# Order of the token tiles in the projection matmuls of a fp32 transformer trunk

## The reference, cut to what matters

```python
def short_conv_mixer(h, w_in, conv_w, w_out):            # layer 0, latent and context tokens
    b_gate, c_gate, v = jnp.split(h @ w_in, 3, axis=-1)
    u = c_gate * v
    up = jnp.pad(u, ((0, 0), (1, 1), (0, 0)))
    z = conv_w[0] * up[:, :-2] + conv_w[1] * up[:, 1:-1] + conv_w[2] * up[:, 2:]
    return (b_gate * z) @ w_out

def swiglu(h, w_in, w_out):                              # both layers; FFN_HIDDEN = 2816
    gate, up = jnp.split(h @ w_in, 2, axis=-1)
    return (jax.nn.silu(gate) * up) @ w_out
```

## Time and profile before

| What | Value |
|---|---|
| Median of 3 runs | 3048.2 us (3044.87 to 3049.11) |
| Profiled execution: span, first to last instruction | 3040.4 us |
| What lies around the span (median less span) | 7.8 us |
| Mean granted TensorE clock over the span | 0.982 |
| TensorE matmul busy | 2898.9 us, 95% |
| VectorE busy | 1954.0 us, 64% |
| ScalarE busy | 866.6 us, 29% |
| GpSimd busy | 921.6 us, 30% |
| conv and ffn0 steps lie at | about 101 to 1481 us of the span |

### The profile page before, as it was taken

How to read it: one execution, slowest core, us unless ns; L and a number is a source line. 1 busy time by engine, 2 the same in 40 slices (tenths; PEclk the granted TensorE clock), 3 DMA queues, 4 the chain that set the end, 5 groups by cost and what they waited for, 6 DMA issues and landing times.

```text
span 3040.4 us, 45152 instructions
## 1 busy us (share of the span) xinstructions
PE 2898.9 (95%) x15546; PEld 2431.6 (80%) x15546; DVE 1954.0 (64%) x3260; ACT 866.6 (29%) x1537; POOL 921.6 (30%) x615
## 2 busy tenths in 40 slices
PE   4999999999999999999999899999798999999997
PEld 2888887788888888888789788888676878888885
DVE  3776775776667666744551566666614887777777
ACT  3211111411111111111241466666623222222222
POOL 1112111111111111112111344545421456565652
PEclk7999999999999999999999899999999999999998
DMA  7122214022221222111055565555640111111111
GB/s 295 46 66 83 72 55 93 32 65 75 72 78 57 78 77 78 52 42 41 35 154 130 151 177 155 168 151 146 191 144 28 42 42 48 55 48 55 48 55 63
DMA packets 178773, 269.43 MB, mean 89 GB/s; under 512 B 70656, under 2 KB 122880, under 8 KB 178688
## 3 DMA queue, kind: packets, MB, share of 16 engines
q1 hardware_dynamic: 178688, 268.32, 28.8%
HBM read 222.13 MB, written 50.07 MB: 90 GB/s over the span
## 4 chain that ended last, share of the span: by engine, by line
PE 78%; DVE 9%; issue 5%; ACT 3%; DMA 3%; POOL 1%; SPq 1%; DVEq 0%; ACTq 0%; POOLq 0%
PE psum L797 33%; PE psum L835 20%; PE psum L1167 5%; PE psum L1025 5%; PE psum L980 4%; PE psum L1079 2%; PE psum L1048 2%; PE psum L823 2%; PE psum L1062 2%; DVE residual L1724 1%; DVE prod_lo L2086 1%; DMA o_dram<-o_st_lo 1%; PE psum L884 1%; DVE part L2080 1%; PE psum L728 1%
## 5 line engine op out<-in xcount | busy, mean ns | idle before, releaser
L1724 DVE SCALAR_TENSOR_TENSOR residual<-psum,modulation,residual 128x512 f32<-128x512 f32 (+1 forms) x1072 | 715.6, 688 | 584.7 <-PE psum L835 581.4
L2174 POOL TENSOR_TENSOR w_lo<-raw,w_hi 128x1024 fp32r<-128x1024 f32 x158 | 396.6, 2521 | 1484.5 <-ACT w_hi L1217 1481.8
L835 PE MATMUL psum<-prod_hi,w_hi 128*128 128x512 f32 (+1 forms) x1072 | 403.6, 377 | 21.8 <-DVE residual L1724 7.3
L797 PE MATMUL psum<-act_hi,w_hi 128*128 128x512 f32 (+1 forms) x1608 | 405.4, 359 | 6.2 <-POOL w_lo L2192 4.3
L797 PE MATMUL psum<-act_lo,w_hi 128*128 128x512 f32 (+1 forms) x1608 | 405.3, 359 | 0.0
L797 PE MATMUL psum<-act_hi,w_lo 128*128 128x512 f32 (+1 forms) x1608 | 405.0, 358 | 0.0
L835 PE MATMUL psum<-prod_hi,w_lo 128*128 128x512 f32 (+1 forms) x1072 | 395.7, 369 | 0.0
L835 PE MATMUL psum<-prod_lo,w_hi 128*128 128x512 f32 (+1 forms) x1072 | 394.9, 368 | 0.0
L1217 ACT ACTIVATE w_hi<-raw 128x1024 fp32r<-128x1024 f32 x158 | 165.8, 1062 | 712.1 <-PE psum L797 607.3
L797 PEld LDWEIGHTS psum<-act_hi,w_hi 128*128 128x128 f32 x1608 | 284.5, 188 | 61.1 <-issue 4.9
L797 PEld LDWEIGHTS psum<-act_hi,w_lo 128*128 128x128 f32 x1608 | 268.0, 188 | 47.1
(11 more groups left out here) (205 smaller groups left out, 5148.6 us busy)
## 6 DMA issues: line engine op xcount, KB each, us to landing
raw<-ffn_panels SPq DMA_DIRECT2D x132, 512.0 KB, 3.8
mod_in<-mod_rest SPq DMA_DIRECT2D x64, 384.0 KB, 3.1
raw<-conv_panels SPq DMA_DIRECT2D x32, 512.0 KB, 5.3
mod_raw<-mod_panels SPq DMA_DIRECT2D x24, 512.0 KB, 8.2
more_row<-mod_panels SPq DMA_DIRECT2D x48, 256.0 KB, 2.8
k_hi<-k_dram SPq DMA_DIRECT2D x32, 320.0 KB, 5.7
k_lo<-k_dram SPq DMA_DIRECT2D x32, 320.0 KB, 7.3
v_st<-v_dram SPq DMA_DIRECT2D x32, 320.0 KB, 7.1
```

The costliest lines, as they stand in the source:

```text
L797: mm = pe.matmul(psum[:, bank + b, 0:tn], w[:, s, kb, :], acts[h][:, kb, t0:t0 + tn], start=(kb == 0 and n == 0), stop=(kb == KB - 1 and n ...
L835: mm = pe.matmul(psum[:, 6 + r % 2 if bank is None else bank, 0:tn], w[:, s, ob, :], h[:, t0:t0 + tn], start=(n == 0), stop=(n == 2))
L1724: dve.scalar_tensor_tensor(out=residual[:, ob, t0:t0 + tn], in0=psum[:, 6 + r % 2 if bank is None else bank, 0:tn], scalar=modulation[:, g ...
L2174: pool.tensor_tensor(panel(w_lo, s), raw[:, s], panel(w_hi, s), ALU.subtract).then_inc(lo_done[s], 1)
```

## The change

In `project` the loop over channel blocks is run twice: first for the two 512-column tiles (`numbered[:len(LAT)]`), with the out pieces and what else `extra` issues behind each channel block as before, and then for what is left (`numbered[len(LAT):]`), the 256-column context tile, with nothing between. Over `LAT` the second pass is empty. The waits on `early_lo` and `lo_done` in the first pass stay where they were in the channel-block order. The number of matmuls, their operands and their accumulation order within a tile are the same. The other engines' programs are not touched.

```diff
-                for kb in range(KB):
-                    if early is not None and kb == 0:
-                        pe.wait_ge(early_lo, early)
-                    elif early is not None and kb == KQ:
-                        pe.wait_ge(lo_done[s], base[phase][s] + i + 1)
-                    for n, (w, h) in enumerate(((w_hi, 0), (w_hi, 1), (w_lo, 0))):
-                        for b, (t0, tn) in enumerate(tiles):
-                            mm = pe.matmul(psum[:, bank + b, 0:tn], w[:, s, kb, :], acts[h][:, kb, t0:t0 + tn],
-                                           start=(kb == 0 and n == 0), stop=(kb == KB - 1 and n == 2))
-                            if kb == KB - 1 and n == 2:
-                                mm.then_inc(ready, 1)
-                    extra(kb)
+                numbered = list(enumerate(tiles))
+                for some in (numbered[:len(LAT)], numbered[len(LAT):]):
+                    for kb in range(KB):
+                        if early is not None and some[:1] == numbered[:1] and kb == 0:
+                            pe.wait_ge(early_lo, early)
+                        elif early is not None and some[:1] == numbered[:1] and kb == KQ:
+                            pe.wait_ge(lo_done[s], base[phase][s] + i + 1)
+                        for n, (w, h) in enumerate(((w_hi, 0), (w_hi, 1), (w_lo, 0))):
+                            for b, (t0, tn) in some:
+                                mm = pe.matmul(psum[:, bank + b, 0:tn], w[:, s, kb, :], acts[h][:, kb, t0:t0 + tn],
+                                               start=(kb == 0 and n == 0), stop=(kb == KB - 1 and n == 2))
+                                if kb == KB - 1 and n == 2:
+                                    mm.then_inc(ready, 1)
+                        if some[:1] == numbered[:1]:
+                            extra(kb)
```

## The result

The changed kernel takes 3065.94 us (median of 4 runs, 3065.45 to 3068.55) against 3048.65 (4 runs, 3044.87 to 3051.82) for the kernel before: a ratio of 1.0062, 95% interval 1.005 to 1.0074. By the two medians that is 17.3 us slower, by the ratio 18.9. The forecast was 3062.6, in a range of 3051 to 3077.

What follows compares the result with a forecast made beforehand. TensorE, with matmuls busy for 95% of the span, was taken to set the time. Terms of -13.2, +24.5, +2 and +1.1 us sum to +14.4, giving 3062.6 us on the median, range 3051 to 3077.

Steps and rivals of the forecast that it cites:

- Term 1: Matmul spacing in conv and ffn0: 1512 triples (two wide matmuls, one narrow) each 0.0087 us shorter, 13.2 us less.
- Rival B: Matmul spacing in conv and ffn0 doesn't change: sum +27.6 us, 3076 us; chance 0.10.
- Term 2: Out piece 11 of 16 group steps, after projection b's start E: wait 1.88 instead of 0.35 us, 24.5 us more.
- "line 1853 runs through": Bound of Term 2: GpSimd holds only line 1856's instructions; wait at piece 11 about 1.4 us, 16.8 us more.
- Rival A: Head of projection b: GpSimd doesn't hold VectorE, 3039 us, chance 0.09; halfway, only line 1856 held, 3055 us, 0.11.
- Term 3: Conv step starts: projection a waits for the late context copy, 0.45 us more in six steps; together 2 us more.
- Term 4: Start of ffn0 steps: piece 0's cover for w_lo of panel 2 shrinks but holds; last step 1.1 us more.
- Rival C: The clock falls in the new idle stretch of 1.7 us in group steps: 26 us, sum 3089 us; chance 0.08.
- the 7.8 us: Whole kernel before: median of the runs lies 7.8 us above the profiled span of 3040.4 us.

Runs made afterwards that it cites:

- grouped: Kernel before the change, one pass kept, but each channel block takes its six wide matmuls and then its three narrow ones: 3028.5 us, ratio 0.9945.
- the cover given back: Changed kernel with the out pieces of the last channel block issued behind the context pass instead of ahead of it: 3063.03 us, ratio 1.0046.

## Why the prediction was right, and where its sizes were off

**What bounds the kernel, and the sign.** Right. TensorE sets the time, its instructions are unchanged, and the result is spacing gained against waits added.

**Term 1, spacing (13.2 less).** Mis-sized. A plain step fell by 0.35 us, not 0.42; over its 48 triples that is 0.0073 each and 1512 x 0.0073 = 11.0 us. Start to start, two wide matmuls take 0.457 in the changed kernel's plain steps and not the 0.453 of the attention's output; the narrow ones are at 0.120 as forecast. Why wide ones are a little slower here is open. Rival B (no gain) is out: in the plain step nothing else was touched. The formula that rival B took from the Trainium skill (TensorE: Matmul & The Clock Gate, "Back-to-back issue gap") makes the gap depend on width alone, and the page calls it the gap of an isolated matmul. For the streams here the traces contradict it, with 0.582 us a triple before, 0.577 after and 0.575 to 0.576 grouped.

**Term 2, piece 11 (24.5 more).** The mechanism is right in each moment: `w_lo` forecast from E + 1.61 to 4.02 and measured at 1.61 to 4.01, modulation from E + 2.31 against 2.34, piece 11 at E + 6.34 against 6.33, its wait 1.88 against 1.84. Both halves of its growth, the later `w_lo` and the earlier due time, stand in the prediction's working. The cost was a little higher. A group step grew by 1.29 net; with the spacing gain of 0.35 taken out that is 1.64, not 1.53, and 16 x 1.64 = 26.2. The wait itself grew by 1.49. Starting again behind it costs some 0.1 us, but it cost that before as well. The other 0.15 is lost at piece 21, in every group step of the changed kernel and in none before. The prediction had cost the second placement of four modulation instructions, behind piece 17, at nothing. Behind it, the add of piece 19 ends at 1082.54, when piece 21 wants that bank, and the first matmul of piece 21 is followed after 0.34 us; before, it was free 0.8 us ahead and the distance was 0.23. The trace names no releaser for so short a wait; the times fit. DVE and PE after, then before:

```profile
1081.13 1.41 DVE L1727 SCALAR_TENSOR_TENSOR residual<-psum,modulation,residual 128x512 f32<-128x512 f32 x2
1082.59 0.50 PE L838 MATMUL psum<-prod_hi,w_hi 128*128 128x512 f32 x1
1082.93 0.40 PE L838 MATMUL psum<-prod_lo,w_hi 128*128 128x512 f32 x1
...
1019.43 1.40 DVE L1724 SCALAR_TENSOR_TENSOR residual<-psum,modulation,residual 128x512 f32<-128x512 f32 x2
1021.65 0.40 PE L835 MATMUL psum<-prod_hi,w_hi 128*128 128x512 f32 x1
1021.88 0.39 PE L835 MATMUL psum<-prod_lo,w_hi 128*128 128x512 f32 x1
```

So the nothing was 16 x 0.15 = 2.4 us. That is the whole shortfall of this term, 1.7, and more; the wait at piece 11 itself grew by a little less than forecast. The lower bound, "line 1853 runs through", is out: these are held like the others (0.74 alone, 2.21 beside `w_lo`). Rival A is out with it. The rule from the Trainium skill (SBUF — State Buffer, "SBUF: two separate sides"), that the second to start waits for the whole instruction of the first, held in every run where the two met: 0.21 to 0.22 us from the end of `w_lo` to that of the held instruction.

**Term 3, conv start (2 more).** The wait grew by 0.44, as worked out (0.45), in six steps 2.6. Left out was that the two wide tiles end early and let VectorE's products go ahead of `w_lo`. One wait even shrank by it, that of the last conv step's out pieces, from 5.21 to 4.44 us.

**Term 4, start of an ffn0 step.** Right: no group or plain step waits for `w_lo` of panel 2. In the last step it does, by 0.94 and some start-up, 1.10 as forecast:

```profile
1487.96 0.50 PE L838 MATMUL psum<-prod_hi,w_hi 128*128 128x512 f32 x1 [0.94 <-POOL w_lo L2177]
```

**The sum.** -11.0 + 26.2 + 2 + 1.1 = +18.3 by the terms as measured, against +14.4 forecast. In the traces the stretch from the first to the last modulation sums, which holds 15 group steps, is 19.3 us longer after than before. The runs give 17.3, interval 15.2 to 22.6. So term 1 gained 2.2 us less and term 2 cost 1.7 more than forecast, both in the same direction; the forecast didn't come near by errors that cancel.

**Rival C, the clock.** Out. In windows around that stall (length in us, busy PE, PEld, DVE, ACT, POOL with counts, PEclk, DMA share, GB/s) the granted clock stays at 1.00, its upper level of 2.4 GHz, and over the stretch of the last 15 group steps its mean is 1.00 in both kernels:

```profile
1066.00:1070.00 4.00, 2.39 (x11) 1.64 (x9) 4.00 (x7) 0.00 (x0) 1.75 (x1) 1.00 0.00 0
1070.00:1076.00 6.00, 5.93 (x29) 5.01 (x30) 4.43 (x9) 0.00 (x0) 0.00 (x0) 1.00 0.22 66
```

**The span and the median.** The prediction put the 7.8 us between them on the median. That was harmless for the sum, but it named as something around the span what was an execution 6 us below the others; the direct difference of the first two spans, 26.4 us, would have overstated the loss by half.

## What to carry to other kernels

When an order within a group of matmuls is changed, ask which result comes last and what is queued behind it, and which work now comes sooner to an engine that hasn't got faster. Here the matmuls gained 11 us and the waits lost 26: about half through one tile that was ready 1.4 us later, about half because the out pieces were no longer spaced by the narrow matmuls. The same gain was to be had with no tile late, by grouping the widths inside each channel block.

A wait that is taken away shows what is late next. Two of the repairs, the cover given back and projection c in one pass, exchanged one wait for another of about the same length or more. Before such an edit, write down every instruction of VectorE that is moved next to one of GpSimd's, in both directions.

## What was not expected of the hardware

- A TENSOR_SCALAR with a single SBUF tile as input is held by GpSimd's two-input instruction until that ends: 0.74 us for two alone, 2.21 beside it. The prediction had kept it possible that it wasn't.
- Narrow matmuls aren't all alike: in the grouped kernel's plain steps the first narrow one is followed after 113 ns, the next after 119 and 120, while a narrow one between wide ones in the kernel before is at 121. The 512-column ones are at 228.5 ns among their like. In the kernel before they are at 232 with a narrow one next and 230 just behind one; in the grouped kernel it is 227 with a narrow one next and 233 just behind one. So it isn't a fixed price for each change of width. The cause is open.
- Two executions of the same kernel differ by 6 us in their spans, with equal steps from the second of ffn0 on: the difference lies in the start, the stretch between conv and ffn0, ffn0's first step and, the other way, attention.
